# Reordering two engines' queues in the SSD stage of a fused layer stack, and swapping two PSUM banks

## The reference

```python
z, xbc, dt = jnp.split(u @ w_in, [...], axis=-1)
xbc = silu(causal_depthwise_conv(xbc, conv_w, conv_b))      # 4 taps
xs, bm, cm = jnp.split(xbc, [...], axis=-1)                 # 4 groups of 8 heads
xdt = xs * dt[..., None]
cb = einsum('bclgn,bcsgn->bcgls', cm, bm)                   # per chunk of 128 tokens
y_diag = einsum('bcgls,bcgrls,bcsgrp->bclgrp', cb, segsum_exp(da), xdt)
states = einsum('bclgn,bclgr,bclgrp->bcgrpn', bm, decay_to_end, xdt)
y_off = einsum('bclgn,bcgrpn,bclgr->bclgrp', cm, prev, exp(a_cs))
y = (y_diag + y_off + d_skip * xs) * silu(z)                # then RMS norm per group, @ w_out
```

## Time and profile before

| what | value |
|---|---|
| median of 3 runs | 2113.44 us (2112.35 to 2115.14) |
| the profiled execution's own time | 2113.44 us |
| its span, first to last instruction | 2111.6 us |
| PE busy | 1975.9 us (94% of the span) |
| DVE busy | 1072.6 us (51%) |
| ACT busy | 871.8 us (41%) |
| POOL busy | 173.3 us (8%) |
| mean granted TensorE clock | 0.967 of full speed |

### The profile page before, as it was taken

The page is one execution under the profiler, slowest core; times in us unless marked ns, Lnnn a source line. Parts: engine busy times, 40 slices in busy tenths (PEclk is TensorE's granted clock), DMA queues, the critical chain, the costliest instruction groups (busy, mean ns, idle before and its releaser), DMA issues.

```text
span 2111.6 us, 26519 instructions
## 1 busy us (share of the span) xinstructions
PE 1975.9 (94%) x9594; PEld 1572.8 (74%) x9594; DVE 1072.6 (51%) x1891; ACT 871.8 (41%) x1734; POOL 173.3 (8%) x137
## 2 busy tenths in 40 slices
PE   7999999979999999899898689999999879989998
PEld 6788887878888887688888577888887655447773
DVE  4666666355344344467677554343446342035643
ACT  5665664253333225366575534233334220114430
POOL 0110110030000003001010040000004000001100
PEclk9999999999999999999999799999999979988999
DMA  5131124313232220413121122222231212110010
GB/s 186 41 100 60 41 80 156 123 61 120 80 118 81 96 103 20 120 42 79 40 80 41 60 88 93 80 103 96 81 118 45 86 53 100 64 40 1 0 40 40
DMA packets 116542, 161.31 MB, mean 76 GB/s; under 512 B 6021, under 2 KB 57059, under 8 KB 116451
## 3 DMA queue, kind: packets, MB, share of 16 engines
q1 hardware_dynamic: 115155, 155.38, 22.1%
q0 software_dynamic: 1296, 4.72, 0.6%
HBM read 157.98 MB, written 2.10 MB: 76 GB/s over the span
## 4 chain that ended last, share of the span: by engine, by line
PE 82%; DVE 9%; ACT 5%; issue 2%; DVEq 1%; ACTq 1%; DMA 0%; SPq 0%; POOLq 0%; POOL 0%
PE psum L885 42%; PE psum L660 8%; PE psum L986 7%; PE psum L1141 4%; PE psum L625 4%; PE psum L848 3%; PE psum L1222 2%; PE psum L1176 2%; PE psum L1018 2%; PE psum L1189 2%; PE psum L965 1%; PE psum L809 1%; DVE z_lo L1782 1%; DVE w_lo L1992 1%; ACT fT L1279 1%
## 5 line engine op out<-in xcount | busy, mean ns | idle before, releaser
L1992 DVE TENSOR_TENSOR w_lo<-slot,w_hi 128x512 fp32r<-128x512 f32 x304 | 214.0, 719 | 377.4 <-ACT w_hi L1448 377.4
L1448 ACT CAST w_hi<-slot 128x512 fp32r<-128x512 f32 x304 | 183.7, 620 | 446.9 <-PE psum L885 446.2
L885 PE MATMUL psum<-f_hi,w_hi 128*128 128x512 f32 (+1 forms) x576 | 214.4, 372 | 21.4 <-issue 8.5
L885 PE MATMUL psum<-f_lo,w_hi 128*128 128x512 f32 (+1 forms) x576 | 213.5, 371 | 0.0
L885 PE MATMUL psum<-f_hi,w_lo 128*128 128x512 f32 (+1 forms) x576 | 213.2, 370 | 0.0
L885 PE MATMUL psum<-w_hi,hid_hi 128*128 128x512 f32 x512 | 199.5, 390 | 0.0
L885 PE MATMUL psum<-w_hi,hid_lo 128*128 128x512 f32 x512 | 199.2, 389 | 0.0
L885 PE MATMUL psum<-w_lo,hid_hi 128*128 128x512 f32 x512 | 199.2, 389 | 0.0
L885 PEld LDWEIGHTS psum<-f_hi,w_hi 128*128 128x128 f32 x576 | 111.7, 194 | 40.2 <-issue 8.9
L625 PE MATMUL psum<-con,arena 128*128 128x128 f32 (+2 forms) x710 | 106.1, 288 | 23.4 <-ACT arena L1695 8.2
L885 PEld LDWEIGHTS psum<-f_hi,w_lo 128*128 128x128 f32 x576 | 111.7, 194 | 17.6
(11 more groups left out here) (309 smaller groups left out, 4118.9 us busy)
## 6 DMA issues: line engine op xcount, KB each, us to landing
slot<-in_w_mlp SPq DMA_DIRECT2D x128, 512.0 KB, 5.5
slot<-in_w_ssd SPq DMA_DIRECT2D x32, 512.0 KB, 5.6
slot<-in_w_hgrn SPq DMA_DIRECT2D x32, 512.0 KB, 6.6
slot<-in_w_ssd_out SPq DMA_DIRECT2D x16, 512.0 KB, 6.2
slot<-in_w_gate SPq DMA_DIRECT2D x16, 512.0 KB, 5.2
gb<-in_w_ssd SPq DMA_DIRECT2D x8, 512.0 KB, 8.3
slot<-in_w_hgrn_out SPq DMA_DIRECT2D x8, 512.0 KB, 5.3
slot<-in_w_mla SPq DMA_DIRECT2D x8, 512.0 KB, 5.5
```

What stands on the lines that cost most here:

```text
L885: m = pe.matmul(psum[:, bank[c], cols or slice(0, HALF)], a, m_, start=opens and k == 0 and n_pass == 0, stop=closes and k == KD - 1 and n ...
L1448: act.copy(w_hi[:, k, :], as_k(slot_of(stage, n))[:, k, :]).then_inc(high_made, 1)
L1992: dve.tensor_tensor(w_lo[:, k, :], as_k(slot_of(stage, n))[:, k, :], w_hi[:, k, :].bitcast(F32), ALU.subtract).then_inc(low_made, 1)
```

## The change

Three things are changed, all in the SSD stage, in each of the four groups (the moved unit "bc" only in the first three, which have a successor). In the bank table, xt 1 and acs 5 change places: xt 1 goes to bank 4, behind CB, and acs 5 to bank 5, behind BT. On ACT the split of the next group's "bc" moves from behind `exp_diff(7)` to ahead of `exp_diff(4)`. On DVE `taps(5)` moves behind `weights(0)` to `weights(3)`, and the low part of the next group's "bc" moves from behind `weights(7)` to ahead of `weights(4)`. No instruction is added or removed.

```diff
-                           (("xt", 1), 5), (("acs", 5), 4), (("z", 0), 2), (("xt", 2), 6), (("acs", 6), 7), (("z", 1), 3),
+                           (("xt", 1), 4), (("acs", 5), 5), (("z", 0), 2), (("xt", 2), 6), (("acs", 6), 7), (("z", 1), 3),
@@ ScalarE
                 silu(5, ("x", 3), cv[:, 2, :])
+                if g + 1 < S_GROUPS:
+                    ssd_high(g + 1, "bc")
                 exp_diff(4)
                 exp_diff(5)
                 x_out(2)
                 exp_diff(6)
                 x_out(3)
                 exp_diff(7)
-                if g + 1 < S_GROUPS:
-                    ssd_high(g + 1, "bc")
@@ VectorE
                 x_dt(0)
-                taps(5, ("x", 3), 4 * g + 3)
                 for j in range(4):
                     weights(j)
+                taps(5, ("x", 3), 4 * g + 3)
                 x_dt(1)
+                if g + 1 < S_GROUPS:
+                    ssd_low(g + 1, "bc")
                 weights(4)
                 weights(5)
                 x_dt(2)
                 weights(6)
                 x_dt(3)
                 weights(7)
-                if g + 1 < S_GROUPS:
-                    ssd_low(g + 1, "bc")
```

## The result

The changed kernel takes 2135.6 us (median of 4 runs, 2133.95 to 2136.93), where the kernel before takes 2112.9 in the same set. The ratio is 1.0106, with a 95% interval of 1.0088 to 1.0124: 1.1% slower. The forecast was 2135.1. Its profiled execution is a quick one, 2132.4 us by its own time, with a span of 2130.6, so the spans of the two traces differ by 19.0 us.

A forecast was written before the change was run, and what follows sets the result against it. PE, busy 94% of the span, was taken as the bound. Swap 1.6, stalls 14.4 and clock 5.7 make 21.7 us, added to 2113.44: 2135.1 us, range 2121 to 2139.

The forecast's parts named there:

- Bank swap: At xt 1 and acs 5: four more transposes run behind the wait for CB, 0.40 us per group, 1.6 in all.
- the statement that they keep 3.3: PE's four waits for DVE's mask of CB (line 1880) were to stay at 3.3 us in total.
- Weights beside POOL: On DVE, the first four weights run beside two POOL instructions and lose 1.7 us, bounds 0 to 2.1.
- the rival at 2122.6: DVE not held by POOL among the weights, stalls 1.7 us shorter each, clock likely to hold; chance 0.15.
- The stalls: PE waits at acs 6 for the late release of bank 7: 4.15 us in groups 0 to 2, 1.97 in group 3.
- the 1.5 us of slack: Before the change, exp_diff(4)'s activations release bank 7 1.5 us ahead of PE's need; the change spends this.
- The clock: PE's granted clock falls once behind the stall in each of groups 0 to 2, 1.9 us each, 5.7 in all.
- The bounds of 1.4 to 2.3: Cost in us of one fall of PE's clock, from two falls seen in the trace of the kernel before.
- the remark from below: A clock fall may cost 0: group 0's 1.7 us wait brought none, and group 3's stall is nearer to that.
- 2115.0: Rival: PE is not stalled at acs 6 and only the swap's 1.6 us is paid; chance 0.06.
- What hides nothing: Later on PE's path in the SSD stage, nothing was to absorb the delay.

The follow-up runs named there:

- swap alone: Kernel before with only xt 1 moved to bank 4 and acs 5 to bank 5: 2116.18 us against 2114.57, ratio 1.0006.
- acs 6 in bank 0: Changed kernel with acs 6 put in bank 0 and z 2 in bank 7, orders as changed: 2118.84 us against 2112.3 before, ratio 1.0021.
- bc alone: Kernel before with only the split of bc moved, ahead of exp_diff(4) on ACT and weights(4) on DVE: 2118.01 us against 2114.57, ratio 1.0015.
- changed, again: The changed kernel run once more without any edit: 2136.32 us against 2112.3 for the kernel before, ratio 1.0102.
- taps alone: Kernel before with only taps(5) moved behind the first four weights: 2127.43 us against 2114.57, ratio 1.006.
- POOL later: Changed kernel with POOL's first pair of instructions in each group held until the silu of x3: 2127.85 us against 2112.3 before, ratio 1.0062.
- changed, PE kept at work: Changed kernel with ten extra throw-away matmuls between x_turn(2) and acs 6 in groups 0 to 2: 2132.48 us against 2112.3 before, ratio 1.0087.

## Why the prediction was right

**Bank swap, 4 x 0.40 = 1.6.** The mechanism stands, the size is 0.50 a group, 2.0 us in all. The waits show 5.4 us in four places in place of 3.3, so the statement that they keep 3.3 was wrong. Four more transposes stand behind the release, which makes 0.4, and PE starts 0.15 us behind the end of DVE's mask (231.82 + 0.68 = 232.50, to 232.65), where it was 0.06. What the 0.09 is was not tried. Moreover, the clock falls behind the longer wait of group 0 (2.3 us recorded) in six of seven profiles that have the swap, all but the changed kernel's first, and in none of the four that have this wait without the swap, where it is at most 1.75 us. The fall costs 1.6 us in "swap alone" and 0.9 in "acs 6 in bank 0", where the small wait at acs 7 takes up the rest; elsewhere the stall at acs 6 swallows it, since its end is set by ACT: group 0 of the changed kernel grew by 6.08 us without that dip and by 6.11 with it. The prediction did not have this.

**Weights beside POOL, 1.7.** Measured 4.19 - 2.49 = 1.70, and gone when POOL is held back. This row decided between the forecast and the rival at 2122.6.

**The stalls, 3 x 4.15 + 1.97.** With the clock held, a group grows by 4.53 (4.52, 4.58 and 4.48 in groups 0 to 2), against the forecast 0.40 + 4.15; with the measured swap it leaves 4.03 for the stall. Group 3 grew by 88.85 - 86.44 = 2.41 (from its 24 transposes to the end of the stage), forecast 0.40 + 1.97 = 2.37. That bank 7 was the place is shown by the run with acs 6 in bank 0, and the 1.5 us of slack by "bc alone". The parts don't add up. Without their three dips of 1.5 they make 10.1 + 2.2 + 2.0 = 14.3, and the whole with the clock held makes 16.0: the slack of 1.5 us that taps and bc each have to themselves can be spent only once, while a PE that comes later through the swap stands less. Worked out with the terms of the prediction, these two come to 3 x 1.5 - 4 x 0.4 = 2.9 us, where 1.7 was measured. Most of the difference is that each part alone measured about 0.1 us a group above its working (2.5 for 2.37, 0.74 for 0.68, 0.50 for 0.40), and the whole did not.

**The clock, 3 x 1.9 = 5.7.** The changed kernel's groups 0 to 2 grew by 6.08, 6.12 and 7.16 us; less the same groups with the clock held, the falls cost 1.6, 1.5 and 2.7, together 5.8. The bounds of 1.4 to 2.3 were a little narrow. The mechanism is shown; that the sum came out within 0.1 us is in part luck, since 1.9 was the middle of two unlike cases and none of the three falls costs it. What failed is the remark from below: one wait of 1.7 us without a fall was taken to say that a stall near 2 us keeps the clock. The trace of before has a fall behind a shorter one: the fall within 37 to 60 us is right behind this wait of 1.46 us at block x0, which follows 16 small matmuls:

```profile
38.62 0.47 PE L660 MATMUL psum<-in_hi,ring 128*128 128x512 f32 x1 [1.46 <-DVE x_lo L1782]
```

Twelve of the 13 profiles have this fall. The changed kernel's first has none, and there PE came earlier to `x_turn(0)` and stood 1.27 us for ACT instead. From block x0 to `x_turn(1)` it took 30.27 us without the fall and 30.28 with it in "changed, again", so this fall costs the stage nothing. How long a wait is does not settle by itself whether the clock falls; what else does was not tried. In "taps alone" it fell in two of four such stalls, in "POOL later" in two of two in groups 1 and 2. Group 3 of the changed kernel kept it in both profiles, with 1.75 us of recorded wait, but the rivals at 2122.6 and 2115.0 were priced too low by that: the runs nearest to them added 12.33 us to the stage for 9.2, and 3.53 for 1.6. For the total of the changed kernel it didn't matter.

**What hides nothing.** No later wait of PE in the stage gave time back, as was said: line 804 waits 0.9 to 1.0 us in every variant.

Left open is the scatter outside the stage. The rest of the span is 1748.4 to 1753.2 us in the profiles, whatever the kernel, and the growth of a median differs from that of its stage by up to 4.2 us: "changed, PE kept at work" has the stage at +16.0 and its median 20.2 above before. So the forecast's 0.5 us from the measured median is closer than these medians can tell; the stage, 21.77 for 21.7, is the better test. Falls of the clock at the many other idle stretches are a possible source of the scatter; it wasn't tested.

## What to carry to other kernels

Before moving work ahead of an instruction on a side engine, look for what that instruction releases and how much earlier than needed it does so: here 1.5 us between the release of a PSUM bank and its next claim was the whole allowance, and 3.9 + 2.2 us were put in front of it. Ask also which engine will run beside the moved work: four DVE instructions took 1.7 times as long in POOL's company. Where PE has to stand, as here for 1.5 to 3.8 us, price a fall of the clock too, and look for another bank before another order.

## What the runs showed of the hardware

- The granted clock fell at waits of PE with a recorded idle of only 2.1 to 2.3 us amid dense matmuls, in some groups and executions of the same code and not in others, and in twelve of 13 profiles behind one of 1.46 us that follows small matmuls. At the stalls of acs 6 a fall cost 1.5 to 2.7 us. Ten matmuls of throw-away work within a stall of 4 us kept the clock at 1.00 and made the stage 5.75 us shorter.
- Four DVE instructions with both inputs in SBUF, back to back, were held by POOL's two for 1.70 us. The starts show two of the four stretched, 1.47 and 1.44 us for 0.6, and POOL was held too (1.05 to 1.24 and 1.04 to 1.48 us). The three taps, which read PSUM, took 2.39 us beside the same POOL instructions and 2.38 us without them.
